# A mixture-of-experts loop: two of four pairs of experts take their rows by a 0/1 matmul, the other two by gather and VectorE transposes

## What is computed

```
def moe_ffn(h, p):
    t = h.reshape(b * s, d)
    scores = jax.nn.sigmoid((t @ p['w_router']).astype(jnp.float32))
    ...
    combine = jnp.einsum('tk,tke->te', w, jax.nn.one_hot(e_idx, N_EXPERTS, dtype=jnp.float32)).astype(h.dtype)
    gte = jnp.einsum('td,edf->tef', t, p['w_gate_e'])
    upe = jnp.einsum('td,edf->tef', t, p['w_up_e'])
    routed = jnp.einsum('tef,efd->td', jax.nn.silu(gte) * upe * combine[:, :, None], p['w_down_e'])
    shared = (jax.nn.silu(t @ p['w_gate_s']) * (t @ p['w_up_s'])) @ p['w_down_s']
```

## Time and profile before

| | us |
|---|---|
| median of three executions | 932.84 |
| lowest, highest | 930.03, 932.85 |
| the profiled execution, its own time | 932.54 |
| its span, first to last instruction | 930.8 |
| TensorE busy | 870.0 (93%) |
| VectorE busy | 353.6 (38%) |
| ScalarE busy | 194.6 (21%) |
| GpSimd busy | 128.7 (14%) |
| moved by DMA | 324.72 MB, mean 349 GB/s |

### The profile page before, as it was taken

How to read it: one execution, slowest core, us unless ns; L and a number is a source line. 1 busy time by engine, 2 the same in 40 slices (tenths; PEclk the granted TensorE clock), 3 DMA queues, 4 the chain that set the end, 5 groups by cost and what they waited for, 6 DMA issues and landing times.

```text
span 930.8 us, 18059 instructions
## 1 busy us (share of the span) xinstructions
PE 870.0 (93%) x7470; PEld 564.3 (61%) x7470; DVE 353.6 (38%) x800; ACT 194.6 (21%) x506; POOL 128.7 (14%) x155
## 2 busy tenths in 40 slices
PE   5999999997889899899899999999999998989897
PEld 3788888875666677657755555554555554545452
DVE  2315580037344689336223322322233222222225
ACT  2000110316222398033111111111111110101012
POOL 0000000022476000000302211101011110101100
PEclk9999999999999999999999999999999999999998
DMA  9966766727499939999999999999999999999993
GB/s 367 398 225 245 283 256 239 301 91 264 151 339 340 383 120 321 384 419 385 362 422 418 423 418 423 418 422 422 416 424 418 422 419 422 420 424 419 423 373 134
DMA packets 58564, 324.72 MB, mean 349 GB/s; under 512 B 13849, under 2 KB 22922, under 8 KB 37938
## 3 DMA queue, kind: packets, MB, share of 16 engines
q1 hardware_dynamic: 47154, 305.43, 81.8%
q0 software_dynamic: 9568, 17.93, 5.6%
q10 hardware_dynamic: 1760, 0.20, 0.2%
HBM read 326.55 MB, written 7.45 MB: 359 GB/s over the span
## 4 chain that ended last, share of the span: by engine, by line
PE 42%; DMA 17%; SPq 2%; DVE 2%; ACT 1%; issue 1%; POOLq 0%; DVEq 0%; ACTq 0%
PE bank L2148 17%; PE bank L2086 9%; PE bank L2097 4%; DMA slot_b<-in_w_e 4%; DMA x<-in_w_e 4%; DMA row_of<-in_w_e 4%; PE bank L1955 3%; PE bank L2062 2%; SPq L1806 1%; DMA ring<-in_w_units 1%; DMA out_ssm_s<-st 1%; DMA ac<-x_row 1%; PE bank L2158 1%; PE bank L2132 1%; SPq L1814 1%
## 5 line engine op out<-in xcount | busy, mean ns | idle before, releaser
L423 PE MATMUL bank<-h,ring 128*128 128x264 f32 x608 | 138.4, 388 | 0.5 <-PE bank L423 0.3
L423 PEld LDWEIGHTS bank<-h,ring 128*128 128x128 f32 x608 | 114.6, 190 | 21.9 <-issue 2.6
L2571 DVE TENSOR_TENSOR con<-scales_of,bank 64x256 f32<-64x256 f32 x64 | 27.2, 425 | 236.7 <-ACT scales_of L2342 236.7
L1826 POOL DMA_INDIRECT xg<-tok_rows,tab_g x32 | 36.1, 1129 | 364.4 <-PE bank L2062 315.1
L2086 PE MATMUL bank<-ring,ht 128*32 128x512 f32 x320 | 72.5, 595 | 10.1 <-DMA x<-in_w_e 5.2
L2342 ACT ACTIVATE scales_of<-bank 64x256 f32<-64x256 f32 x64 | 24.2, 378 | 274.0 <-PE bank L2148 274.0
L2148 PE MATMUL bank<-done_out,xt 128*64 128x256 f32 x704 | 78.4, 381 | 0.1
L2148 PE MATMUL bank<-ring,xt 128*64 128x256 f32 x672 | 77.2, 382 | 0.4 <-ACT xt L2331 0.4
L2526 DVE COPY sq<-bank 128x512 f32<-128x512 f32 x64 | 44.3, 692 | 73.5 <-PE bank L2086 73.5
L2148 PEld LDWEIGHTS bank<-done_out,xt 128*64 128x64 f32 x704 | 50.5, 137 | 30.1 <-issue 7.0
L2148 PEld LDWEIGHTS bank<-ring,xt 128*64 128x64 f32 x672 | 46.8, 137 | 35.0 <-issue 14.1
(11 more groups left out here) (471 smaller groups left out, 1281.2 us busy)
## 6 DMA issues: line engine op xcount, KB each, us to landing
ring<-in_w_units SPq DMA_DIRECT2D x25, 2048.0 KB, 11.4
done_out<-in_w_e SPq DMA_DIRECT2D x22, 2048.0 KB, 29.5
ring<-in_w_e SPq DMA_DIRECT2D x20, 2048.0 KB, 28.7
slot_b<-in_w_e SPq DMA_DIRECT2D x11, 2048.0 KB, 30.5
slot_f<-in_w_e SPq DMA_DIRECT2D x10, 2048.0 KB, 29.8
ring<-in_w_e SPq DMA_DIRECT2D x19, 1024.0 KB, 30.8
slot_b<-in_w_e SPq DMA_DIRECT2D x10, 1024.0 KB, 30.2
done_out<-in_w_e SPq DMA_DIRECT2D x10, 1024.0 KB, 28.7
```

The costliest lines, as they stand in the source:

```text
L423: mm = pe.matmul(bank[:, t % NB, 0:T], w[:, j, k, :], h[:, k, :], start=(k == 0), stop=(k == KD - 1))
L1826: pool.indirect_dma_start(xg[q % AHEAD][:, :], None, tok_rows, bass.IndirectOffsetOnAxis(ap=tab_g[:, q:q + 1].bitcast(U32), axis=0), bound ...
L2571: dve.tensor_tensor(hh[e % 2][:, :], sg[e % 2][:, :], bank[LB:2 * LB, 4 + e % 2, 0:FE], ALU.mult).then_inc(hh_ready, 1)
```

## The change

- **Selection (pairs q with q % 4 = 0 or 1).** `h2` gets memory of its own and stays. VectorE computes each token's place in each expert's list from a running count, which TensorE makes by a product with the triangular constant `before` (two products, `pos_done`), and compares it with a constant row of places: `sel`, a 0/1 matrix of 128 tokens x 4 experts x 28 places per tile. A `burst` of 16 products, `h2` columns against `sel`, writes the turned rows of four experts at once, and ScalarE copies them to `xt` (`take_rows`), which now holds four experts. The first burst is ahead of the loop, seven more stand in the pairs 3, 7, ..., 27.
- **Fetched pairs (q % 4 = 2 or 3).** They are gathered as before, into the one buffer `xg` that is left, and VectorE turns them into `xt` (`turn_rows`, L2605): 8 instructions per expert, each 32 partitions x 8 x 32. `turn_rows` of TensorE is gone. 16 of 32 row gathers are gone. The sample tokens' rows come into `xg` once, by 8 more transposes ahead of the loop (L2055), a copy and four small DMAs.
- `half_out` moves from VectorE to ScalarE.
- **Order.** Weight table, weight gather 0 and row gather 2 now follow each other on GpSimd. `w_sd` waits for the routing weights instead of the stored `h2`.
- **Gate/up 5.** 2560 of its 4096 columns (1.31 MB) are loaded in the state stage, right after the first two broadcast rows; the rest where all of it was.
- The rest moves small tiles to other memory and belongs to the path for experts with more tokens than slots.

The diff, cut to its core:

```diff
+++ SP, state stage
                         load_row(0)
                         load_row(1)
+                        sp.dma_start(slot_f[:, EARLY_GU:GU], io["w_e"][5][:, EARLY_GU:GU]
+                                     ).then_inc(small_in, 16)
                         sp.wait_ge(y_done6, 2)
+++ SP
-                        load_gu(sp, 5)
+                        sp.dma_start(gu_at[5][:, 0:EARLY_GU], io["w_e"][5][:, 0:EARLY_GU]).then_inc(gu_in[5], 16)
...
-                        sp.wait_ge(own_in, 1)
+                        sp.wait_ge(own_cols, 2)
                         load_dn(sp, 5)
-                        sp.wait_ge(rows_stored, 32)
+                        sp.wait_ge(wgt_ready, 1)
                         sp.dma_start(w_sd[:, :, :].rearrange("p k c -> p (k c)"), io["w_e"][EXTRA][:, GU:EW]).then_inc(w_sd_in, 16)
+++ GpSimd
+            def fetched(q):
+                return q % 4 >= 2
+
+            def nth_fetched(q):
+                return q // 4 * 2 + q % 2
+
             def gather(pool, q):
-                if q >= AHEAD:
-                    pool.wait_ge(xt_done, 2 * (q - AHEAD) + 2)
-                pool.indirect_dma_start(xg[q % AHEAD][:, :], None, tok_rows,
+                if nth_fetched(q):
+                    pool.wait_ge(turned_ready, 2 * nth_fetched(q))
+                pool.indirect_dma_start(xg[:, :], None, tok_rows,
...
-                        gather(pool, AHEAD)
+                        pool.wait_ge(own_in, 16 * 4)
+                        pool.wait_ge(rows_stored, 32)
                         pool.wait_ge(tab_stored, 32)
-                        gather_weights(0)
-                        gather_weights(1)
-                        gather(pool, AHEAD + 1)
-                        for q in range(2, NPAIR):
-                            if q + AHEAD < NPAIR:
-                                gather(pool, q + AHEAD)
+                        for q in range(NPAIR):
+                            if q % 4 == 2:
+                                gather(pool, q + 1)
                             gather_weights(q)
+                            if q % 4 == 0:
+                                gather(pool, q + 2)
+++ TensorE
+                        def burst(n, i):
+                            l, ks = i // 2, range(KD // 2 * (i % 2), KD // 2 * (i % 2 + 1))
+                            b = (BANKS if n else FIRST_BANKS)[i]
+                            q = 4 * n - 1
+                            if n == 0:
+                                pe.wait_ge(sel_ready, l + 1)
+                            elif i == 0:
+                                pe.wait_ge(sel_ready, n + 2)
+                                pe.wait_ge(hh_ready, 2 * q + 2)
+                            elif i < 3:
+                                pe.wait_ge(y_ready, 2 * q - 2 + i)
+                            if i == 3:
+                                pe.wait_ge(xt_ready, 4 * n + 1)
+                            for k in ks:
+                                at = k % (KD // 2) * P
+                                out = bank[:, b, at:at + P].rearrange("p (e s) -> p e s", e=EG)[:, :, 0:LS]
+                                mm = pe.matmul(out, h2[:, l, k * P:(k + 1) * P], sel[:, l, :, :], start=True, stop=True)
+                            mm.then_inc(xt_done, 1)
+++ TensorE, gate_up
-                            pe.wait_ge(xt_ready, e // 2 * 2 + 2 if e else 1)
+                            if fetched(e // 2):
+                                pe.wait_ge(turned_ready, 2 * nth_fetched(e // 2) + e % 2 + 1)
+                            else:
+                                pe.wait_ge(xt_ready, e // 8 * 4 + 4)
+++ TensorE, loop
-                            if q + 1 < NPAIR:
-                                for h in range(2):
-                                    turn_rows(q + 1, h)
+                            if q % 4 == 3 and q + 1 < NPAIR:
+                                for i in range(4):
+                                    burst((q + 1) // 4, i)
                             turn_inner(q)
+++ VectorE
+                        def turn_rows(q, h):
+                            if h == 0:
+                                dve.wait_ge(x_in, 16 * (nth_fetched(q) + 1))
+                            dve.wait_ge(gu_done, 2 * q - 3 + h)
+                            for l in range(2):
+                                at = h * LB + l * HB
+                                rows = xg[at:at + HB, :].rearrange("p (k r c) -> p r k c", k=KD, r=4)
+                                for r in range(4):
+                                    ins = dve.transpose(xt[32 * r:32 * r + 32, :, 2 * q % EG + h, l, :], rows[:, r, :, :])
+                            ins.then_inc(turned_ready, 1)
+++ VectorE, loop
                                 dve.tensor_tensor(hh[e % 2][:, :], sg[e % 2][:, :], bank[LB:2 * LB, 4 + e % 2, 0:FE], ALU.mult).then_inc(hh_ready, 1)
+                                if q % 4 == 1 and e % 2 == 0:
+                                    turn_rows(q + 1, 1)
+                                if q % 4 == 2:
+                                    turn_rows(q + 1, e % 2)
                             if q:
                                 weight_matrix(q - 1)
-                                half_out(2 * q - 2)
-                                half_out(2 * q - 1)
...
                             if q:
                                 add_own(q - 1)
+                            if q % 4 == 0:
+                                turn_rows(q + 2, 0)
+                            if q % 4 == 1 and q + 3 < NPAIR:
+                                dve.wait_ge(xt_done, q + 3)
+                                select(slice(0, 2), q // 2 + 2).then_inc(sel_ready, 1)
                             if q == 0:
                                 own_weights()
```

More of the change, by code:

```diff
@@ L85 @@
 GU = KD * 2 * FE
+AT_SLOT_F = AT_SAMP - 4 * GU
+EARLY_GU = 3 * 2 * FE
 EW = GU + 2 * D
@@ L2015, in _ @@
                         turn_half(0, 1)
+                        pe.wait_ge(x1_ready, 2)
+                        for k in range(KD):
+                            mm = pe.transpose(bank[0:TS, k // 4, k % 4 * P:(k % 4 + 1) * P], h2t[:, k, TP:T], ident)
+                        mm.then_inc(srow_done, 1)
                         pe.wait_ge(score_ready, 2)
@@ L2493, in _ @@
                         route(2, 2, 3)
+                        for l, a in ((0, 0), (1, 2)):
+                            places(l, a)
+                            select(slice(l, l + 1), 0).then_inc(sel_ready, 1)
+                        keys_of(0)
+                        keys_of(2)
                         take_lists()
```

232 lines of the change are left out of this document (127 added, 105 removed).

## The result

The changed kernel takes **961.64 us** (median of six executions, 957.9 to 963.45). The kernel before, run beside it, takes 931.37 us (930.03 to 932.85). The ratio is 1.032, 95% interval 1.030 to 1.034: slower by 30 us, far above the forecast of 933.5 us and outside its range, whose upper end was 942. The profiled execution took 957.93 us, its span is 956.2 us. It began the MoE part 2.9 us earlier than the profiled execution before (389.1 us against 392.0).

A forecast was written before the change was run, and what follows sets the result against it. The weight stream bounds the loop, TensorE having 15.3 us of slack. DMA side -0.2, TensorE +8.7 - 28.6 + 25.8 + 10.5 - 15.3 = +1.1; the later decides: 933.6, adjusted to 933.5 us, range 928.0 to 942.0.

The forecast's parts named there:

- VectorE's turns set the pair: Slower rival in the expert loop: H = 3.2 gives 940.2 us, H = 3.5 gives 947.4; chance 0.28.
- the likeliest case: Whole kernel: no change within 0.3%, the forecast and its neighbours, 930 to 935.6 us; chance 0.38.
- seven waits of 3H - 7.3 in the C pairs = 10.5 us: Combine in each later C pair waits 1.5 us for the weight matrix, seven times.
- C pairs: Fetched pairs with q % 4 = 2; A, B are the selected pairs (0, 1), D the other fetched one (3).
- H: VectorE's time to turn one half of a fetched pair, 8 transposes: 2.9 us, bounds 2.4 and 3.5.
- The gather: D's row gather, in the chain through pairs B, C, D: lands 10.4 us after issue, the median.
- The first round: Pairs 0 to 3, late weights and rows: pair 3 starts at 500.2 instead of 491.52, +8.7 us.
- the case H = 3.5: Upper bound for turning a half: C waits of 3.2 us, 22.4 in all, first round +10.6, 947.4 us.
- DMA side: Weight stream: -7.4 for gathers, +3.2 later start, +5.0 idle, -1.0 in the tail, together -0.2 us.
- the faster rival: H is 2.4, no wait in C, DMA decides: -4.2, 928.3 us; chance 0.28.
- The sum of the rival whose gathers cost DMA half: Gathers slip between weights, saving DMA only 3.7 us: DMA side +3.0, 935.5 us; chance 0.06.
- The sign that I had set for a time above 938 us: In the loop: no TensorE waits for weights and C pairs over 15 us mean the forecast is wrong.

The follow-up runs named there:

- Mending it: Row gather 2 issued as soon as the lists stand, own_w copied before the first turn: 950.28 us on the changed kernel, 925.13 us on the spread kernel.
- the spread kernel: Changed kernel with both fetched pairs' turns spread over pairs A and C and their gathers issued earlier: 928.65 us, ratio 0.998.
- the kernels that set the stream free again: Changed kernel with half the transposes, 924.78 us; spread turns with first round mended, 925.13 us; the latter without the early part of gate/up 5, 925.06 us.
- with the matrix first: Changed kernel with the weight matrix made ahead of the turn of D's second half: 941.17 us, ratio 1.010.

## Why the prediction was wrong

The mechanism stood in it, as the rival "VectorE's turns set the pair", with the right chain and the right place of the wait, but without the lower clock behind the wait. It got 0.28 and the likeliest case 0.38. The step that failed is the term "seven waits of 3H - 7.3 in the C pairs = 10.5 us": it is 36.4 us, some 26 of delay and 10.5 of lower clock.

- **H.** Forecast 0.365 us a transpose, H = 2.9; measured 0.45, H = 3.6. I took the pace of a VectorE copy whose successor starts 0.35 us after it, and bounded it above by the copy's full duration. The upper bound was right: these transposes run end to end. With it 3H - 7.3 = 3.5 us, seven times is 24.5, and TensorE's waits in the trace are 24.1. So the formula gives the sum with the right input, but not the single groups, which wait 1.6 to 4.6 us. It also left out a second limit, the 1.6 us that the order on VectorE costs even with the gather out of the chain. The Trainium skill (VectorE: DVE Perf Modes, The three transpose paths), by which I had estimated 0.44 us, was the nearer source; the trace has 0.436 busy and 0.45 to the next. I had set it aside for a row of another kind of instruction.
- **The gather.** Taken at the median of 10.4; in the long groups it took 11.4. It is in series, so it counts in full, +1.0, which the groups with extra work on TensorE give back (2.9 us in the group with the shared expert's products).
- **The clock.** Not in the prediction at all: behind a long wait the combine ran at 1.2 GHz, some 10.5 us in the seven groups and some 4 in the first round. That is why even the case H = 3.5, 947.4 us, lay 10 below the profile. Its 22.4 us of waits were 3.5 too few without the clock, and its first round of +10.6 was 3.9 too much; these two nearly cancel.
- **The first round.** Pair 3 was forecast at 500.2, +8.7, and starts at 498.22, +6.7. Counted from each kernel's own loop start it was forecast 7.7 later and is 8.9 later. That the size is right is luck. The prediction had waits of 4.5 (own_w), 2 (hh of expert 3) and 4 us (pair 2's combine), 10.5 together; the trace has 5.1, 0.9 and 1.6, 7.5 together, and some 4 us of lower clock that I had not forecast. Mending it gave 3.5 us on the spread kernel (928.65 to 925.13) and 11 on the changed one.
- **The loop's start.** 62.0 us after the MoE part's start against 61.3 before, +0.7; forecast +1.0. The burst: 3.76 us, forecast 3.7.
- **DMA side.** Forecast -0.2 with H = 2.9, 928.3 for the faster rival. It did not come to bear here, but in the kernels that set the stream free again it did: 924.8 to 925.1 us, 3 us below the forecast. The sum of the rival whose gathers cost DMA half is 0.5 us off: with 3.7 added to -0.2 it is +3.5, 936.0 us, not 935.5.
- **Early part.** Forecast no cost and no gain; measured twice, and neither run contradicts it, within 3 to 4 us. The half copies moved to ScalarE: forecast off the path; the trace shows no wait of TensorE for them before the tail. That was not tried by itself.
- **The sum.** 933.6 us, + 25.9 for the C pairs (36.4 instead of 10.5), - 2.0 for pair 3's start in absolute time, + 0.5 for bursts, gives 958.0 against 957.93 in the profile; the median lies 3.7 higher. The early start of the profiled execution (2.9 us) and its short wait for own_w would both do that; the other executions left no trace, so it stays open. That the sum meets the profile to 0.1 us is partly luck: its 36.4 is 0.9 above the 35.5 that the difference of the two kernels leaves, and it does not hold the stretch from pair 31 to the last instruction, which is 0.8 us longer than before.

The sign that I had set for a time above 938 us, no waits for weights and C pairs of over 15 us, is what the trace shows. The range ended at H = 3.2, although the text itself gave 3.5 as a bound of equal standing and the time 947.4 for it. Nothing but the pace of a different instruction spoke for the lower value, so the range should have gone to that bound.

## What to carry to other kernels

When work moves to an engine that is idle for two thirds of the time, its load says nothing; what counts is where in its list the new instructions stand and who waits for the one behind them. Here the kernel with 256 transposes is 30 us slower than the one before in one order and no slower in another: put them behind the last thing that the bound engine waits for, and issue a single-buffered gather as early as its buffer allows. A wait of a few microseconds on TensorE is to be priced with the slower work behind it, and an unseen instruction at its upper bound when it stands three times in series.

## What the runs showed of the hardware

- VectorE's transposes of 32 partitions x 256 columns in float32, from SBUF to SBUF, take 436 ns and follow each other after 0.45 us, though a copy of 256 columns from PSUM is followed after 0.35.
- After 0.97 + 3.63 us of TensorE's idleness the granted clock was 0.50 for the next 3.7 us and at 1.00 again from 625.4, 8 us later. After the 5.08 us for own_w it was 0.54 over 10.4 us. After waits of 1.6 us the combine took 1.99 us, so it did not fall; with the matrix first it fell behind each of three waits of 2.1 us, and not behind three of 1.5 to 1.8. Filled with work without use, the same place kept 1.00, and the kernel was faster by 6.4 us.
- Four products, alternating between the two halves of the rows (combine, eight records), take 1.83 us; the same shape on one half only takes 0.43 us a record, so 3.4 us for eight records.
